# Second attention of a two-block kernel: one 512-column score product over both key sets, bias added in the bank

## The reference, cut to what matters

```python
s_loc = jnp.einsum('bwhd,biwjhd->bhwij', q_r, k_win).astype(jnp.float32) * scale + bias
s_ctx = jnp.einsum('bwhd,bchd->bhwc', q_r, k_ctx).astype(jnp.float32) * scale
s_all = jnp.concatenate([s_loc.reshape(B, H, GRID_W, n_loc), s_ctx], axis=-1)
prob = jax.nn.softmax(s_all, axis=-1)
...
return (jnp.einsum('bhwij,biwjhd->bwhd', p_loc, v_win)
        + jnp.einsum('bhwc,bchd->bwhd', p_ctx, v_ctx))
```

## Time and profile before

| | us |
|---|---|
| median of 3 runs | 1457.29 (1457.16 to 1457.7) |
| the profiled execution | 1455.16 |
| its span | 1453.4 |
| stretch of the attention in it | about 503 to 566 |
| PE busy in the span | 1379.7 (95%) |
| DVE, ACT, POOL busy | 949.6, 775.3, 458.7 |

### The profile page before, as it was taken

The page is one execution under the profiler, slowest core; times in us unless marked ns, Lnnn a source line. Parts: engine busy times, 40 slices in busy tenths (PEclk is TensorE's granted clock), DMA queues, the critical chain, the costliest instruction groups (busy, mean ns, idle before and its releaser), DMA issues.

```text
span 1453.4 us, 22196 instructions
## 1 busy us (share of the span) xinstructions
PE 1379.7 (95%) x8932; PEld 1251.2 (86%) x8932; DVE 949.6 (65%) x1510; ACT 775.3 (53%) x1251; POOL 458.7 (32%) x247
## 2 busy tenths in 40 slices
PE   6999899999986999799799999999999999999997
PEld 6898789999865777799799999988888888888886
DVE  5676777887788756498976666555465555555555
ACT  5465745444444355445379999544454444545443
POOL 1530013545363101688742221111211211221113
PEclk9999999999997999999999999999999999999999
DMA  7553256777885822557555445566666566666665
GB/s 237 172 151 95 94 173 216 257 242 255 273 283 188 308 88 87 189 160 210 175 157 156 145 146 155 194 202 211 214 207 203 188 212 216 205 203 199 199 214 195
DMA packets 190325, 278.86 MB, mean 192 GB/s; under 512 B 9184, under 2 KB 120544, under 8 KB 189968
## 3 DMA queue, kind: packets, MB, share of 16 engines
q1 hardware_dynamic: 184640, 266.19, 56.2%
q10 hardware_dynamic: 5184, 10.02, 1.8%
q0 software_dynamic: 400, 1.25, 0.3%
HBM read 266.41 MB, written 11.01 MB: 191 GB/s over the span
## 4 chain that ended last, share of the span: by engine, by line
PE 60%; DVE 6%; DMA 1%; ACT 1%; POOL 1%; issue 1%; DVEq 0%; SPq 0%; ACTq 0%
PE bank L679 16%; PE bank L646 16%; PE bank L684 8%; PE bank L651 8%; PE bank L946 4%; PE bank L619 3%; PE bank L623 1%; PE bank L864 1%; PE bank L883 1%; DMA sb_raw<-w_in 1%; DVE sb_lo L1344 1%; DMA sb_raw<-peer_uT 1%; PE bank L871 1%; PE bank L905 1%; ACT sb_hi L980 0%
## 5 line engine op out<-in xcount | busy, mean ns | idle before, releaser
L1970 POOL TENSOR_TENSOR sb_lo<-sb_raw,sb_hi 128x1024 fp32r<-128x1024 f32 x149 | 378.6, 2548 | 821.3 <-ACT sb_hi L980 821.1
L980 ACT ACTIVATE sb_hi<-sb_raw 128x1024 fp32r<-128x1024 f32 (+2 forms) x427 | 443.1, 1048 | 269.6 <-DMA sb_raw<-peer_v 68.4
L1344 DVE TENSOR_TENSOR sb_lo<-sb_raw,sb_hi 128x1024 fp32r<-128x1024 f32 (+2 forms) x279 | 391.2, 1413 | 234.0 <-ACT sb_hi L980 232.5
L646 PE MATMUL bank<-sb_act_hi,sb_hi 128*128 128x256 f32 x1632 | 407.7, 288 | 8.2 <-ACT sb_hi L980 7.1
L646 PE MATMUL bank<-sb_act_lo,sb_hi 128*128 128x256 f32 x1632 | 402.2, 284 | 0.0
L646 PEld LDWEIGHTS bank<-sb_act_hi,sb_hi 128*128 128x128 f32 x1632 | 314.4, 193 | 11.0 <-ACT sb_hi L980 5.0
L646 PEld LDWEIGHTS bank<-sb_act_lo,sb_hi 128*128 128x128 f32 x1632 | 315.2, 193 | 1.5
L679 PE MATMUL bank<-sb_hi,sb_hid_hi 128*128 128x512 f32 x600 | 234.2, 390 | 0.9 <-DVE sb_hid_lo L1659 0.9
L651 PE MATMUL bank<-sb_act_hi,sb_lo 128*128 128x256 f32 x1632 | 230.0, 284 | 4.8 <-POOL sb_lo L1970 4.7
L679 PE MATMUL bank<-sb_hi,sb_hid_lo 128*128 128x512 f32 x600 | 234.4, 391 | 0.0
L651 PEld LDWEIGHTS bank<-sb_act_hi,sb_lo 128*128 128x128 f32 x1632 | 210.7, 192 | 5.8 <-POOL sb_lo L1970 5.8
(11 more groups left out here) (329 smaller groups left out, 1445.0 us busy)
## 6 DMA issues: line engine op xcount, KB each, us to landing
sb_raw<-peer_uT SPq DMA_DIRECT2D x128, 512.0 KB, 3.9
sb_raw<-peer_v SPq DMA_DIRECT2D x128, 512.0 KB, 4.9
sb_raw<-w_in SPq DMA_DIRECT2D x52, 512.0 KB, 4.7
sb_ada_w<-ada_wT SPq DMA_DIRECT2D x48, 512.0 KB, 5.6
sb_raw<-w_gate SPq DMA_DIRECT2D x22, 512.0 KB, 3.8
sb_raw<-w_up SPq DMA_DIRECT2D x22, 512.0 KB, 3.6
sb_raw<-w_down SPq DMA_DIRECT2D x22, 512.0 KB, 3.9
sb_raw<-w_out SPq DMA_DIRECT2D x16, 512.0 KB, 3.6
```

What stands on the lines that cost most here:

```text
L646: e.matmul(bank[:, j * T:(j + 1) * T], hi[:, k, j * P:(j + 1) * P], part[:, k0 + k, :], start=i == first_i and j == 0 and k == 0 and part ...
L980: e.activation(flat_of(i, "hi"), flat_of(i, "raw"), ACT.Copy).then_inc(hi_done[i % R], 1)
L1344: e.tensor_tensor(flat_of(i, "lo"), flat_of(i, "raw"), flat_of(i, "hi").bitcast(F32), ALU.subtract).then_inc(lo_done[i % R], 1)
L1970: e.tensor_tensor(flat_of(i, "lo"), flat_of(i, "raw"), flat_of(i, "hi").bitcast(F32), ALU.subtract).then_inc(lo_done[i % R], 1)
```

## The change

`k_T` and `kc_T` come to lie side by side in one buffer, and a view `both_T` takes, for a head, the 256 own and the 256 context keys as 2 x 256 columns. PE does one product of 512 columns for an item into one bank. q is scaled when it is copied out. DVE adds the bias in the bank, in place, and takes the maximum over the bank; ACT's exponential reads the bank and writes the SBUF buffer. ACT's copy of the second half is gone. The bank is freed by the exponential; the slot of a bias block is given back by the maximum of its last item, no longer by the scale-and-add.

```diff
-        q_T, k_T, kc_T = (by_chunk(place(n, 1024)) for n in ("q_T", "k_T", "kc_T"))
+        q_T, keys_of = by_chunk(place("q_T", 1024)), place("k_T", 2048)
+        k_T, kc_T = by_chunk(keys_of[:, 0:1024]), by_chunk(keys_of[:, 1024:2048])
+        both_T = keys_of.rearrange("p (w c t) -> p c w t", w=2, c=4)
...
-                    for part, kk in enumerate((k_T, kc_T)):
-                        bank = take("na", "scores", i, part)
...
-                        e.matmul(bank[:, 0:T], q, kk[lo:lo + 64, h // 2, :], start=True, stop=True).then_inc(*fills("na", "scores", i, part))
-                    for part in range(2):
-                        give("na", "scores", i, part)
+                    bank = take("na", "scores", i)
...
+                    e.matmul(bank[:, :].rearrange("p (w t) -> p w t", w=2), q, both_T[lo:lo + 64, h // 2], start=True, stop=True).then_inc(*fills("na", "scores", i))
+                    give("na", "scores", i)
                 elif what == "turn":
                     bank = take("na", "turn", i)
-                    pe.wait_ge(*att_exp.at("na", i))
+                    pe.wait_ge(*freed("na", "scores", i))
...
                 if j == 2:
-                    heads_out("q", q_T, 4)
+                    heads_out("q", q_T, 4, NA_SCALE)
...
                 if what == "scores":
-                    if i >= 4:
-                        act.wait_ge(*full("na", "turn", i - 4))
-                    act.wait_ge(*full("na", "scores", i, 1))
-                    e.activation(buf[:, T:2 * T], psum("na", "scores", i, 1)[:, 0:T], ACT.Copy, scale=NA_SCALE).then_inc(*gives("na", "scores", i, 1))
...
                 elif what == "exp":
+                    if i >= 4:
+                        act.wait_ge(*full("na", "turn", i - 4))
                     act.wait_ge(*att_max.at("na", i))
-                    e.activation(buf, buf, ACT.Exp, bias=nmax_of[i % 4], accum_out=tot_of[i % 4]).then_inc(*att_exp.inc("na", i))
+                    e.activation(buf, psum("na", "scores", i)[:, :], ACT.Exp, bias=nmax_of[i % 4], accum_out=tot_of[i % 4]).then_inc(*gives("na", "scores", i))
...
+                    if name == "q":
+                        dve.wait_ge(*full(name, i0))
+                        e.tensor_scalar(dst[0:n, i0:i0 + 2, :], by_chunk(psum(name, i0)[0:n, 0:512]), NA_SCALE, None, ALU.mult).then_inc(*gives(name, i0))
...
-                    if i >= 4:
-                        dve.wait_ge(*full("na", "turn", i - 4))
+                    bank = psum("na", "scores", i)
                     dve.wait_ge(*in_slot(blk))
-                    dve.wait_ge(*full("na", "scores", i, 0))
-                    e.scalar_tensor_tensor(buf[:, 0:T], psum("na", "scores", i, 0)[:, 0:T], NA_SCALE, cut_of(blk, "full")[:, 0, o:o + T], ALU.mult, ALU.add).then_inc(*gives("na", "scores", i, 0))
+                    dve.wait_ge(*full("na", "scores", i))
+                    own(e.tensor_tensor(bank[:, 0:T], bank[:, 0:T], cut_of(blk, "full")[:, 0, o:o + T], ALU.add))
                     if h % 2 and qb == NT - 1:
-                        release[blk] = [freed("na", "scores", i, 0)]
+                        release[blk] = [att_max.at("na", i)]
                         let_go.add(blk)
-                    dve.wait_ge(*freed("na", "scores", i, 0))
-                    dve.wait_ge(*freed("na", "scores", i, 1))
-                    max_of("na", i, buf)
+                    max_of("na", i, bank[:, :])
```

More of the change, by code:

```diff
@@ L1029, in norm_out, with copy_out, heads_out @@
                         ins.then_inc(*gives("norm", stage, c2))
-            def copy_out(dst, src, *key):
+            def copy_out(dst, src, *key, scale=1.0):
                 act.wait_ge(*full(*key))
-                e.activation(dst, src, ACT.Copy).then_inc(*gives(*key))
-            def heads_out(name, dst, n_blocks):
+                e.activation(dst, src, ACT.Copy, scale=scale).then_inc(*gives(*key))
+            def heads_out(name, dst, n_blocks, scale=1.0):
                 n = plan_rows[name]
                 for i0 in range(0, n_blocks, 4):
-                    copy_out(dst[0:n, i0:i0 + 2, :], by_chunk(psum(name, i0)[0:n, 0:512]), name, i0)
+                    copy_out(dst[0:n, i0:i0 + 2, :], by_chunk(psum(name, i0)[0:n, 0:512]), name, i0, scale=scale)
             plan_rows = dict(qm=MLA_QK, km=MLA_QK, dq=P, dk=P, q=P, k=P, kc=P)
@@ L1453, in heads_out @@
                 for i0 in range(2, n_blocks, 4):
-                    copy_out(dst[0:n, i0:i0 + 2, :], by_chunk(psum(name, i0)[0:n, 0:512]), name, i0)
+                    if name == "q":
+                        dve.wait_ge(*full(name, i0))
+                        e.tensor_scalar(dst[0:n, i0:i0 + 2, :], by_chunk(psum(name, i0)[0:n, 0:512]), NA_SCALE, None, ALU.mult).then_inc(*gives(name, i0))
+                    else:
+                        copy_out(dst[0:n, i0:i0 + 2, :], by_chunk(psum(name, i0)[0:n, 0:512]), name, i0)
             def pair_lo(name, i0, dst):
```

8 lines of the change are left out of this document (4 added, 4 removed).

## The result

The changed kernel takes 1460.46 us (median of 11 runs, 1457.89 to 1461.37), the kernel before 1457.16 in runs taken beside it (11 runs, 1454.49 to 1458.81). The ratio is 1.0019, with a 95% interval of 1.0010 to 1.0028: 2.8 us slower, 1.5 to 4.1; the medians are 3.3 us apart. A second comparison gave 1.0039 (1.0025 to 1.0052), 5.7 us, though its medians, 1460.57 us of 9 runs against 1457.22 of 27, are only 3.4 us apart. The forecast was 0.6 us slower, 1457.9, with 1459.0 as the upper end. So it is slower for some 2 us more than forecast, by a difference near what can be measured at all. The profiled execution took 1461.33 us, its span 1459.5.

What follows compares the result with a forecast made beforehand. PE was taken to bound the kernel, in the attention through its own chain of pieces. Products -0.3, lost savings +0.1 and a new stall +0.8 gave +0.6 us on 1457.29: 1457.9 us, range 1455.3 to 1459.0.

Steps and rivals of the forecast that it cites:

- The product: Attention score product on PE: two passes of 512 columns, 0.86 us instead of 0.88, saving 0.02 us an item, 0.3 in all.
- the edges: PE's switches between 64-row score products and 128-row work: forecast to stay; rival had them go, saving 3.2 us, 1454.1, chance 0.03.
- the rival that took this idle for a wait: PE's idle before the attention's transposes is a wait, gone for 13 of 16 items: 2.0 us saved, 1455.9, chance 0.05.
- a bank costs DVE nothing: In the attention, DVE's in-place add in the bank stays near 0.42 us and its maximum from the bank near 0.69.
- The new stall: PE waits 0.8 us before item 5's score product in the attention, for the bank item 3's exponential frees.
- the path written down: Item 3's maximum releases the slot, SP issues 1.1 us later, ACT rounds later, the exponential follows, item 5's bank frees late.
- other held bank: From item 5 on, score products wait for the exponential two items back; forecast no stall, nearest with 1.1 us to spare.
- The bounds 0 and 1.3: Limits in us of the stall before item 5: 0 if the load lands sooner, 1.3 if it takes half a microsecond more.
- the sum: Attention terms: -0.3 products, +0.1 savings lost at two stalls, +0.8 new stall, +0.6 us in all; later stages unchanged; chance 0.84.
- The range: Forecast's own range for the whole kernel, 1455.3 to 1459.0 us, from product savings, stall, bank accesses and the runs' spread.
- The held bank throughout: Rival: late exponentials make PE wait throughout the attention, 0.3 us more for each of 11 items, 1461.2 us, chance 0.04.
- the clock: Rival: stalls lower PE's clock in the attention, some 6 us of work at half speed costing 3, 1460.9 us, chance 0.04.

## Why the prediction was right and wrong

**What held.** The product lasts 1.05 to 1.07 us up to the transposes, where about 1.04 was forecast: the columns alone count, nothing is gained at the edges. Its two passes start 0.53 us apart and not 0.43; the four of before start 0.32, 0.22 and 0.22 apart, so the first pass carries 0.10 us of its own in both kernels. The transposes behind it are still 0.59, without a wait in PE's order, and PE's weight load before them is idle for 11.1 us, all "issue": the rival that took this idle for a wait is out. Add 430 ns (0.42 forecast), maximum 692 (0.69): a bank costs DVE nothing. By an estimate from the 62 cycles of the Trainium skill's page "VectorE: DVE Perf Modes", section on the TRN2 errata, the maximum would be at 0.75; the trace has 0.69. ACT's exponential was left at 0.71 and is 0.68. The new stall came at item 5, by the path written down, and by no other held bank: forecast 0.8, measured 0.87 and 0.71 in the two traces, 0.68 in the mean of nine. The bounds 0 and 1.3 held too: 0.16 to 1.08, with the landing of that one load. From item 0's product to the start of the output projection the two traces have 0.8 and 0.6 us more, where the sum said 0.6. So the sum was right for the attention.

**What failed** is the last sentence of the sum: "The stages behind follow PE, whose chain resumes at once, so they pass this on unchanged." It holds for a delay. It does not hold for a program that is shorter by 80, 16 and 7 instructions: the stages behind got other neighbours on the DMA engines. 0.4 us were lost at 602 to 611 us, some 1.3 over 735 to 905, together more than twice the sum. The 1.3 us is the softer of the two numbers (above). The range had the same hole: its upper end was built from the stall and the bank accesses, all inside the attention, and so missed a loss outside.

**The rivals.** The held bank throughout (1461.2) and the clock (1460.9) gave times near the one measured and are both wrong as causes: the chain has one exponential, at item 5, and the attention's granted clock is 1.00. The granted clock was low for longer in the first trace of after, from 594.2 to 604.5 us, and by DVE's marks the stretch from 568 to 603 us was no longer for it (0.01 us). PE itself came 0.6 us later to the wait for the query copy, and waited 0.94 us there instead of 1.14: what holds it is the load. Over whole runs the mean granted clock is 0.984 in either kernel. A time that fits is no sign of a mechanism that does.

## What to carry to other kernels

Where a kernel runs with loads that land just in time, any edit that changes how many instructions an engine has moves every later packet of its program, and the time can change in stages that the edit does not touch; here it went up by some 2 us. So compare stage by stage, and tell an edit's own effect from that of its length by padding the program back with idle waits, ahead of the edit and in an idle stretch. And where a buffer's release moves later, follow the load that it lets go through the queue of the engine that takes it: what stands behind that instruction, and what is held until then, is where the stall appears.

## What the runs showed of the hardware

- Programs come by DMA beside the data: one packet for every 257 instructions of PE (71, 1.16 MB in the run), 0.9 to 2.4 us each by the trace, and smaller ones, of 8 KB (nine in ten of them 0.3 to 0.6 us, a few up to 1.5), for the other engines.
- While the DMA engines are full, an 8 KB packet makes a 1 MB load land 0.4 to 0.6 us later (7.50 to 7.69 in eight traces; in nine without a packet it lands after 7.07 to 7.11). A 16 KB packet of PE made it 8.49, in one trace.
- A PE packet beside a load and a store goes with a load that takes 0.5 us more in the mean, 0.2 in the median, than the same load without one (108 loads).
- A wait that is already met takes about 0.05 us on PE (two in an instruction of 0.11) and 0.04 on ACT (224 in 8.8 us). It costs nothing where the idle stretch is longer than all of them; on ACT and DVE at 566 to 578 us 32 and 14 of them cost 0.3 to 0.6 us.
- An exponential from a bank takes 682 ns where one from SBUF takes 714; DVE's maximum is the same from either (692 and 686).
